# Shift and scale of the adaptive norm as dot products on VectorE over turned weights, in a four-layer fp32 kernel

## The chip, the cores and the metric

One core of one Trainium2 chip. The metric is the device time of one execution in microseconds (us), as the median of several runs.

## The reference, cut to what matters

Four layers follow one another on x of 256 x 1024 in fp32: layer 0 (stick-breaking attention and an S5 mixer), layer 1 (gated linear attention, GLA), and two hybrid layers (dilated attention and retention), called layers 2 and 3 here. Only the hybrid layers are modulated by a vector c of 1024 elements:

```python
c_act = jax.nn.silu(c)
for l in range(DEPTH):            # DEPTH = 2: layers 2 and 3
    mod = c_act @ w_ada[l] + b_ada[l]          # w_ada[l]: 1024 x 3072
    shift, scale, gate = jnp.split(mod, 3, axis=-1)
    h = rmsnorm(x, norm_w[l]) * (1.0 + scale[:, None, :]) + shift[:, None, :]
    proj = h @ w_in[l]
    ...
    x = x + gate[:, None, :] * (merged @ w_out[l])
```

Neither c_act nor w_ada depends on x, so the three parts of mod can be computed at any time before their use: shift and scale before the layer's first projection, the gate before its residual.

## The kernel before, in words

All large products use a split of fp32 in two: a matrix W is WH + WL, with WH = W rounded to the matmul's fp32r form and WL = W - WH, and likewise the activations (HTh, HTl or YTh, YTl). A product is three matmuls: high by high, low by high, high by low. The weights come in 306 **pieces** of 256 rows by 512 columns (512 KB; some of layer 1 have 336 or 352 columns). SP loads a piece into one of five RAW buffers; ScalarE copies it to WH (`hi`, line 1046), VectorE subtracts to WL (`lo`, line 1523), TensorE multiplies (`half`, lines 593 to 605; `split_half`, lines 631 to 633, where a layer opens or closes). WH and WL have three buffers each: `hi(n)` waits until TensorE has read piece n-3, and runs two pieces ahead.

The clock of the whole program is the half piece, here a **step**: piece n is steps 2n and 2n+1. Each engine is written as one loop over the steps, and tables (`AT_...`) say at which step an engine does a side job. All engines thus keep one order, and an engine waits where another is late. SP's loop is set against the same steps. Steps up to 107 are layer 0, from 108 layer 1; layers 2 and 3 each have 216 steps, counted from 0 again within the layer. A side job on VectorE at a step stands ahead of that step's `lo`.

The modulation is such a side job. Its weights are read as they lie, 128 rows (of the 1024) by 512 columns at a time, 256 KB:

- A **step of the modulation** multiplies a 128x512 block of w_ada by a column of c_act (one number per partition) and adds it to an accumulator of 128x512. Eight steps make a column group (cg). Groups 0 and 1 are shift, 2 and 3 scale, 4 and 5 gate.
- In layers 0 and 1, VectorE does groups 0 and 2 for layer 2 (`ada0`, lines 1915 and 1918, 16 steps at `AT_ADA0`), and GpSimd does groups 1 and 3 (`ada`, lines 2372 to 2376, a multiply and an add as two instructions, 16 steps at the same places). SP loads VectorE's blocks (line 2484, three buffers), GpSimd its own (line 2360, two buffers).
- In layers 2 and 3, GpSimd does the rest (`LATER`: both gate groups for layer 2, then all six groups for layer 3), 64 steps at `AT_ADA1`: 48 in layer 2, at steps 8 to 194, and 16 in layer 3, at steps 16 to 66.
- The accumulator's 128 partitions must then be summed. TensorE does it (`ada_sum`). For shift and scale it needs the result as a column: four matmuls with the accumulator as weights and one column of ones (line 814). For the gate it needs the result in all partitions: one matmul with the 128x128 ones as weights (line 817).
- VectorE takes the sums from PSUM and adds b_ada (`ada_out`, lines 1926 to 1936). ScalarE applies shift and scale as it copies the turned norm (`Bcols`, `Acols`).

The rest that the text below names: line 1696/1698, the product behind the GLU; line 1962, the logarithm's part of GLA's decay; line 2001, GLA's gating, whose result TensorE turns (line 556); lines 2068 and 2098/2102, the gating of the attention and of the retention; L1853 is the scan of S5.

```python
AT_ADA0 = (82, 86, 90, 94, 98, 112, 116, 120) + tuple(130 + 4 * i for i in range(8))
AT_ADA0_SUM = {126: (0, 1), 164: (2, 3)}
```

Of the kernel before, what the change touches and what calls it, by code (L numbers as in the profile page):

```python
# [11 lines left out]
ALU = mybir.AluOpType  # L12
# [3 lines left out]
P = 128  # L16
# [93 lines left out]
AT_ADA0_SUM = {126: (0, 1), 164: (2, 3)}  # L110
# [12 lines left out]
LATER = [(0, 4), (0, 5)] + [(1, cg) for cg in range(6)]  # L123
AT_ADA1 = tuple(8 + 29 * g + 3 * k + (0, 20, 50)[g // 2 - 1 if g > 3 else 0] for g in range(8) for k in range(8))
AT_ADA1_SUM = tuple(35 + 29 * g + (0, 20, 50)[g // 2 - 1 if g > 3 else 0] for g in range(8))


def program(nc, t, out):
    ctx = ExitStack()
    with ctx:  # L130
# [21 lines left out]
        CS = sb("CS", [P, 2, 256])  # L152
        SM = sb("SM", [P, 952])
# [97 lines left out]
        ADA = [AH.take(3, 512), AH.take(2, 512)]  # L251
        ADACC = AH.take(2, 512)
# [23 lines left out]
        HN32 = flat(OR).rearrange("p (a b) -> p a b", a=8)  # L276
        SC, PT, ATD = A2.take(1152), A2.take(1152), A2.take(384)
# [126 lines left out]
        def raw_landed(n):  # L404
# [6 lines left out]
         l_fw) = (sem(n) for n in ("l_cols l_ci l_cr l_pos l_br l_tri l_sbm l_gm l_res l_wg l_atm l_dec "  # L411
                                   "l_g0 l_g1 l_fw").split())
        s_ada = [sem(f"ada{i}") for i in range(5)]
# [71 lines left out]
        CACT, CACT_V = events("cact", ["th"]), events("cact_v", ["c"])  # L485

        ADA_V = events("ada_v", range(16))
        ADA_P = events("ada_p", [(l, i) for l in range(2) for i in range(16 + 48 * l)])
        MOD = events("mod", [(0, cg) for cg in range(6)] + [(1, cg) for cg in range(6)])
# [36 lines left out]
        def tensor_program():  # L526
# [277 lines left out]
            def ada_sum(l, cg):  # L804
                late = (l, cg) in LATER
                acc = ADACC2 if late else ADACC[:, cg % 2, :]
                ps = take(("ada", l, cg), MOD.of(l, cg))
                if late:
                    pe.wait_ge(*ADA_P.of(1, 8 * LATER.index((l, cg)) + 7))
                else:  # L810
                    pe.wait_ge(*(ADA_P.of(0, 4 * cg + 3) if cg % 2 else ADA_V.of(4 * cg + 7)))
                if cg < 4:
                    for c in range(4):
                        ins = nc.tensor.matmul(ps[:, c:c + 1], acc[:, 128 * c:128 * c + 128], ONES[:, 0:1], start=True,
                                               stop=True)
# [179 lines left out]
            for time in range(2 * groups["zr"]["at"] + 6, 2 * H0[0]):  # L995
# [5 lines left out]
                if time in AT_ADA0_SUM:  # L1001
                    for cg in AT_ADA0_SUM[time]:
                        ada_sum(0, cg)
# [10 lines left out]
            for l in range(2):  # L1014
                open_layer(2 + l, 2 * H0[l])
                for time in range(6, 216):
                    half(2 * H0[l] + time)
                    if 216 * l + time in AT_ADA1_SUM:
                        ada_sum(*LATER[AT_ADA1_SUM.index(216 * l + time)])
# [24 lines left out]
        def scalar_program():  # L1044
# [22 lines left out]
            def turned(l, ti, r):  # L1067
# [4 lines left out]
                for k in (2 * r, 2 * r + 1):  # L1072
# [4 lines left out]
                    else:  # L1077
                        act.wait_ge(*MOD.of(l - 2, 3))
# [303 lines left out]
            for time in range(2 * groups["zr"]["at"] - 6):  # L1382
# [75 lines left out]
            act.wait_ge(*side("ada", 0, 3))  # L1458
# [58 lines left out]
        def vector_program():  # L1517
# [389 lines left out]
            def ada0(i):  # L1907
                cg, k = 2 * (i // 8), i % 8
                dve.wait_ge(s_ada[i % 3], 16 * (i // 3 + 1))
                w, acc = ADA[0][:, i % 3, :], ADACC[:, 0, :]  # L1910
                if k == 0:
                    dve.wait_ge(*CACT_V.of("c"))
                    if i:
                        dve.wait_ge(*side("ada", 0, cg - 2))
                    ts(acc, w, cact[:, 0:1], None, ALU.mult).then_inc(*dve.mark(ADA_V, i))
                else:
                    dve.wait_ge(*ADA_V.of(i - 1))
                    stt(acc, w, cact[:, k:k + 1], acc, ALU.mult, ALU.add).then_inc(*dve.mark(ADA_V, i))
# [222 lines left out]
            for time in range(2 * groups["zr"]["at"] - 6):  # L2141
# [42 lines left out]
                for b, c in AT_SB_TURN.get(time, ()):  # L2184
                    yt_lo(4 * b + c, "sb", b, c)
# [428 lines left out]
```

## Time and profile before

| what | value |
|---|---|
| median of 3 runs | 1083.46 us (1083.02 to 1085.13) |
| the profiled execution: span from first to last instruction | 1080.6 us; no separate own time is listed for it |
| granted TensorE clock, mean | 0.985 |
| busy: TensorE, VectorE, ScalarE, GpSimd | 1023.9, 703.8, 565.1, 339.1 us |
| read from HBM | 189.07 MB, 176 GB/s over the span |
| loads of w_ada | 80 by GpSimd, 16 by SP, 256 KB each |

The busy time of TensorE is that of pipelined matmuls whose ends overlap: a 128x512 matmul shows as 0.39 us while the next starts after 0.23. Start-to-start distances are the ones to add up. For VectorE, too, an instruction's end overlaps the next one's start by up to 0.1 us. Layer 0 runs to about 227 us, layer 1 to 355, layer 2 to 720.

### The profile page before, as it was taken

To read this page: it belongs to the slowest core of one execution; us is meant where nothing else is said; L and a number is where in the kernel's file an instruction comes from. 1 tells how busy PE (TensorE), PEld (TensorE's weight loads), DVE (VectorE), ACT (ScalarE), POOL (GpSimd) and SP (SyncE) were. 2 spreads that over 40 slices of the span, in tenths; PEclk is the share of its full clock that TensorE was granted. 3 is DMA by queue.
4 is the path that set the end of the run, shared out by engine and by line. 5 is a ranking of instruction groups with operands and counts; after the bars stand their busy time and mean duration, and the time that the engine had idled before them with its cause. 6 is when DMAs were issued, how large, how long until landed. Compare 5 with 4: busy or idle time off the path is not lost.

```text
span 1080.6 us, 15495 instructions
## 1 busy us (share of the span) xinstructions
PE 1023.9 (95%) x6084; PEld 899.1 (83%) x6084; DVE 703.8 (65%) x1072; ACT 565.1 (52%) x872; POOL 339.1 (31%) x349
## 2 busy tenths in 40 slices
PE   5899999989999799999999989989999999999994
PEld 5688889768978589998899878867999889988883
DVE  7884946878767664456476686674545555758665
ACT  6978577547444654455443334555444554334452
POOL 4700060423520164653363555321744000420001
PEclk9899999999999999999999999999999999999997
DMA  7543434757735487765576556646876446644541
GB/s 239 168 123 98 138 96 137 246 181 230 244 127 169 147 265 224 238 197 154 172 217 187 182 157 223 223 123 192 251 215 205 117 120 188 180 150 145 188 161 58
DMA packets 94440, 191.12 MB, mean 177 GB/s; under 512 B 6768, under 2 KB 10096, under 8 KB 94368
## 3 DMA queue, kind: packets, MB, share of 16 engines
q1 hardware_dynamic: 86256, 164.71, 49.7%
q0 software_dynamic: 6960, 22.71, 6.6%
q10 hardware_dynamic: 1152, 2.72, 0.7%
q8 instruction: 48, 0.79, 0.3%
q14 instruction: 24, 0.20, 0.1%
HBM read 189.07 MB, written 1.05 MB: 176 GB/s over the span
## 4 chain that ended last, share of the span: by engine, by line
PE 86%; DVE 7%; ACT 4%; DMA 1%; issue 1%; DVEq 0%; SPq 0%; ACTq 0%
PE G L593 15%; PE G L595 14%; PE G L594 14%; PE G L602 8%; PE G L604 8%; PE G L605 8%; DVE WL L1523 2%; PE B L556 2%; ACT AR L1046 1%; ACT WH L1046 1%; DMA RAW<-in_even_w_in 1%; PE G L631 1%; PE G L633 1%; PE G L632 1%; PE B L905 1%
## 5 line engine op out<-in xcount | busy, mean ns | idle before, releaser
L1523 DVE TENSOR_TENSOR WL<-RAW,WH 128x1024 fp32r<-128x1024 f32 (+2 forms) x306 | 396.4, 1298 | 266.8 <-ACT WH L1046 265.9
L1046 ACT ACTIVATE WH<-RAW 128x1024 fp32r<-128x1024 f32 (+2 forms) x306 | 320.3, 1050 | 289.0 <-PE G L595 148.0
L593 PE MATMUL G<-WH,HTh 128*128 128x512 f32 (+1 forms) x564 | 228.9, 406 | 6.6 <-DVE WL L1523 6.4
L602 PE MATMUL G<-HTh,WH 128*128 128x256 f32 x768 | 219.9, 286 | 0.5 <-DVE HTl L1599 0.5
L595 PE MATMUL G<-WL,HTh 128*128 128x512 f32 (+1 forms) x564 | 219.2, 389 | 0.0
L594 PE MATMUL G<-WH,HTl 128*128 128x512 f32 (+1 forms) x564 | 218.4, 387 | 0.0
L604 PE MATMUL G<-HTl,WH 128*128 128x256 f32 x768 | 217.6, 283 | 0.0
L605 PE MATMUL G<-HTh,WL 128*128 128x256 f32 x768 | 217.5, 283 | 0.0
L602 PEld LDWEIGHTS G<-HTh,WH 128*128 128x128 f32 x768 | 146.8, 191 | 2.4 <-issue 2.2
L604 PEld LDWEIGHTS G<-HTl,WH 128*128 128x128 f32 x768 | 146.9, 191 | 0.9 <-issue 0.7
L605 PEld LDWEIGHTS G<-HTh,WL 128*128 128x128 f32 x768 | 146.8, 191 | 0.0
L2360 POOL DMA_DIRECT2D AR<-in_w_ada x80 | 47.5, 594 | 273.4 <-PE G L595 160.3
L593 PEld LDWEIGHTS G<-WH,HTh 128*128 128x128 f32 x564 | 106.8, 189 | 29.9 <-DVE WL L1523 9.2
L595 PEld LDWEIGHTS G<-WL,HTh 128*128 128x128 f32 x564 | 106.4, 189 | 22.0
L594 PEld LDWEIGHTS G<-WH,HTl 128*128 128x128 f32 x564 | 106.9, 190 | 18.3 <-issue 0.2
L2376 POOL TENSOR_TENSOR AR<-AR 128x512 f32<-128x512 f32 x70 | 118.5, 1693 | 5.8
L593 PE MATMUL G<-WH,YTh 128*128 128x512 f32 x184 | 73.8, 401 | 4.5 <-DVE WL L1523 4.5
L595 PE MATMUL G<-WL,YTh 128*128 128x512 f32 x184 | 72.5, 394 | 0.0
L594 PE MATMUL G<-WH,YTl 128*128 128x512 f32 x184 | 72.3, 393 | 0.0
L2374 POOL TENSOR_SCALAR AR<-AR,SM 128x512 f32<-128x512 f32 x70 | 62.0, 886 | 19.5 <-DMA AR<-in_w_ada 13.9
L1046 ACT ACTIVATE AR<-B 128x512 f32<-128x512 f32 (+5 forms) x83 | 43.0, 546 | 44.9 <-PE B L950 22.4
L2394 POOL TENSOR_TENSOR AR<-AR 128x256 f32<-128x256 f32 x16 | 18.2, 1139 | 139.5 <-DVE AR L2022 138.4
(344 smaller groups left out, 1342.2 us busy)
## 6 DMA issues: line engine op xcount, KB each, us to landing
RAW<-in_w_in SPq DMA_DIRECT2D x176, 512.0 KB, 3.8
RAW<-in_even_w_in SPq DMA_DIRECT2D x40, 512.0 KB, 3.6
AR<-in_w_ada POOLq DMA_DIRECT2D x80, 256.0 KB, 4.1
RAW<-in_odd_w_in SPq DMA_DIRECT2D x16, 512.0 KB, 4.0
RAW<-in_w_proj_ret SPq DMA_DIRECT2D x16, 512.0 KB, 3.6
RAW<-in_w_out SPq DMA_DIRECT2D x16, 512.0 KB, 4.2
RAW<-in_even_w_out SPq DMA_DIRECT2D x12, 512.0 KB, 3.9
AR<-in_w_ada SPq DMA_DIRECT2D x16, 256.0 KB, 5.0
```

The costliest lines, as they stand in the source:

```text
L556: ins = nc.tensor.transpose(ps[:, 128 * k:128 * k + 128], src(ti, j), IDENT)
L593: nc.tensor.matmul(o, xh, wh, start=begins, stop=False)
L594: nc.tensor.matmul(o, xl, wh, start=False, stop=False)
L595: ins = nc.tensor.matmul(o, xh, wl, start=False, stop=ends)
L602: nc.tensor.matmul(o, fh, h_[:, kx, :], start=begins and f % 2 == 0, stop=False, skip_group_check=True)
L604: nc.tensor.matmul(o, fh, l_[:, kx, :], start=False, stop=False, skip_group_check=True)
L605: ins = nc.tensor.matmul(o, fl, h_[:, kx, :], start=False, stop=ends and f % 2 == 1, skip_group_check=True)
L1046: return nc.scalar.activation(out_, ps, ACT.Copy, **kw)
L1523: vt(wl, raw, wh.bitcast(F32), ALU.subtract).then_inc(*dve.mark(LO, n))
L2360: nc.gpsimd.dma_start(dst, wv[:, k, 512 * cg:512 * cg + 512]).then_inc(s_ada[3 + i % 2], 16)
L2374: gts(w, w, cact[:, k:k + 1], 0.0, ALU.mult, ALU.add).then_inc(*pool.tick())
L2376: gtt(acc, acc, w, ALU.add).then_inc(*pool.mark(ADA_P, l, i))
```

## The change

Shift and scale are computed the other way round. The host turns their 2048 columns of w_ada, so that 128 output columns lie on the 128 partitions and the 1024 inputs along the row (`w_ada_t`; one contiguous block of 128x1024, 512 KB). The row of c_act is put in all partitions once (`CB`: a load by GpSimd at step 60, Tanh on ScalarE and one product on VectorE at step 78). Then one instruction on VectorE, a multiply with a sum along the row (`tensor_tensor_reduce`, with b_ada as the start), gives 128 of the outputs as a column, where they are wanted. There are 16 such **dots** for layer 2, at the 16 steps where `ada0` stood, and 16 for layer 3, in layer 2 at steps 27 to 72, every third. GpSimd does the gates alone: 16 steps in layers 0 and 1 (the same places), 16 in layer 3 (steps 26 to 71). TensorE's sums of shift and scale go; those of the gate of layer 2 move to steps 126 and 164. SP loads for all dots, into two buffers; DOT1 uses the place of OR, which is free then. Two waits for the old sum (0, 3), on ScalarE and on GpSimd ahead of layer 2, become waits for the last turn of GLA. The scratch for GpSimd's DMA descriptors is set to 8192 bytes.

```diff
-AT_ADA0_SUM = {126: (0, 1), 164: (2, 3)}
+AT_ADA0_SUM = {126: 4, 164: 5}
...
-LATER = [(0, 4), (0, 5)] + [(1, cg) for cg in range(6)]
-AT_ADA1 = tuple(8 + 29 * g + 3 * k + (0, 20, 50)[g // 2 - 1 if g > 3 else 0] for g in range(8) for k in range(8))
-AT_ADA1_SUM = tuple(35 + 29 * g + (0, 20, 50)[g // 2 - 1 if g > 3 else 0] for g in range(8))
+AT_DOT1 = tuple(27 + 3 * i for i in range(16))
+AT_ADA1 = tuple(216 + 26 + 3 * i for i in range(16))
+AT_ADA1_SUM = {216 + 50: 4, 216 + 74: 5}
+AT_CB = 78
...
-                if cg < 4:
-                    for c in range(4):
-                        ins = nc.tensor.matmul(ps[:, c:c + 1], acc[:, 128 * c:128 * c + 128], ONES[:, 0:1], start=True,
-                                               stop=True)
-                else:
-                    ins = nc.tensor.matmul(ps[:, :], ONES, acc, start=True, stop=True)
-                ins.then_inc(*told("ada", l, cg))
+                pe.wait_ge(*ADA_P.of(l, 8 * cg - 25))
+                nc.tensor.matmul(ps[:, :], ONES, ADACC2 if l else ADACC, start=True, stop=True).then_inc(
+                    *told("ada", l, cg))
...
+                if time == AT_CB:
+                    act.wait_ge(*side("sbo", 1, 1))
+                    act.wait_ge(l_cb, 16)
+                    nc.scalar.activation(DOT0[:, 1, :], CB[:, :], ACT.Tanh, scale=0.5).then_inc(*act.mark(CACT, "row"))
...
-            act.wait_ge(*side("ada", 0, 3))
+            act.wait_ge(*side("yt", "gla", 2))
...
-            def ada0(i):
...
-                    stt(acc, w, cact[:, k:k + 1], acc, ALU.mult, ALU.add).then_inc(*dve.mark(ADA_V, i))
+            def dot(l, i):
+
+                w = (DOT1 if l else DOT0)[:, i % 2, :]
+                dst = (Bcols if i < 8 else Acols)[l][:, i % 8:i % 8 + 1]
+                dve.wait_ge(s_dot[i % 2], 16 * (8 * l + i // 2 + 1))
+                dve.wait_ge(*CACT_V.of("row"))
+                nc.vector.tensor_tensor_reduce(w, w, CB[:, :], 0.5, co[f"b_ada{l}"][:, i:i + 1], ALU.mult, ALU.add,
+                                               dst).then_inc(*dve.mark(DOT, l, i))
+                if i == 15:
+                    dve.wait_ge(*DOT.of(l, 15))
+                    stt(Acols[l], Acols[l], 1.0, co[f"norm_w{l}"], ALU.add, ALU.mult).then_inc(*dve.mark(MOD, l, "c"))
...
+                if time == AT_CB:
+                    dve.wait_ge(*CACT.of("row"))
+                    stt(CB[:, :], DOT0[:, 1, :], 1.0, CB[:, :], ALU.add, ALU.mult).then_inc(*dve.mark(CACT_V, "row"))
...
+                    if l == 0 and step in AT_DOT1:
+                        dot(1, AT_DOT1.index(step))
...
+                if time == 60:
+                    nc.gpsimd.dma_start(CB[:, :], t["c_2"].partition_broadcast(P)).then_inc(l_cb, 16)
...
+            def dot_load(l, i):
+                if i >= 2:
+                    sp.wait_ge(*DOT.of(l, i - 2))
+                elif l:
+                    sp.wait_ge(*HT_LO.of(2, 1, 3))
+                    sp.wait_ge(*ROT_A.of("sin"))
+                    sp.wait_ge(*ROT_V.of("cos"))
+                elif i:
+                    sp.wait_ge(*CACT_V.of("row"))
+                nc.sync.dma_start((DOT1 if l else DOT0)[:, i % 2, :], t["w_ada_t"][l, 128 * i:128 * i + 128, :]).then_inc(
+                    s_dot[i % 2], 16)
...
+                    if at_ in AT_ADA0 and AT_ADA0.index(at_) < 14:
+                        dot_load(0, AT_ADA0.index(at_) + 2)
+                    step = at_ - 2 * H0[0]
+                    if step == AT_DOT1[0] - 3:
+                        dot_load(1, 0)
+                        dot_load(1, 1)
+                    if step in AT_DOT1 and AT_DOT1.index(step) < 14:
+                        dot_load(1, AT_DOT1.index(step) + 2)
...
+    a["w_ada_t"] = a["w_ada_2"][:, :, 0:2048].transpose(0, 2, 1)
+    a["w_ada_g"] = a["w_ada_2"][:, :, 2048:3072]
...
-    nc = _bacc.Bacc("TRN2", target_bir_lowering=False, num_devices=1)
+    nc = _bacc.Bacc("TRN2", target_bir_lowering=False, num_devices=1, dynamic_dma_scratch_size=8192)
```

How the instructions stand then, at two places on VectorE. Names: RAW, WH, WL as above; AR is the large buffer in which the blocks and accumulators lie; SM holds columns. A dot shows as two rows named ISA, the multiply with its sum and the instruction that writes the sum. First the end of layer 0, steps 86 to 98, before:

```order
L1523 TENSOR_TENSOR WL<-RAW,WH 128x1024 x2
L1918 SCALAR_TENSOR_TENSOR AR<-AR,SM 128x512
L1696 SCALAR_TENSOR_TENSOR AR<-AR 128x512
L1698 SCALAR_TENSOR_TENSOR AR<-AR 128x512
L1696 SCALAR_TENSOR_TENSOR AR<-AR 128x512
L1698 SCALAR_TENSOR_TENSOR AR<-AR 128x512
L1523 TENSOR_TENSOR WL<-RAW,WH 128x1024
L2190 TENSOR_TENSOR YTl<-AR,YTh 128x512
```

and with the change (its own line numbers):

```order
L1521 TENSOR_TENSOR WL<-RAW,WH 128x1024 x2
L1911 ISA AR,SM<-AR,CB,SM 128x1024
L1911 ISA SM 128x1
L1694 SCALAR_TENSOR_TENSOR AR<-AR 128x512
L1696 SCALAR_TENSOR_TENSOR AR<-AR 128x512
L1694 SCALAR_TENSOR_TENSOR AR<-AR 128x512
L1696 SCALAR_TENSOR_TENSOR AR<-AR 128x512
L1521 TENSOR_TENSOR WL<-RAW,WH 128x1024
L2178 TENSOR_TENSOR YTl<-AR,YTh 128x512
```

The dot stands where the half-width step stood, ahead of the GLU's product and of the next low half. Second, layer 2 from step 17 on, before:

```order
L1523 TENSOR_TENSOR WL<-RAW,WH 128x1024 x3
L1669 TENSOR_TENSOR CS<-AR 128x256
L1671 TENSOR_SCALAR CS<-CS 128x256
L1523 TENSOR_TENSOR WL<-RAW,WH 128x1024 x6
L1936 TENSOR_TENSOR AR<-B,AR 128x512
L1523 TENSOR_TENSOR WL<-RAW,WH 128x1024 x15
```

and with the change, up to the third dot:

```order
L1521 TENSOR_TENSOR WL<-RAW,WH 128x1024 x3
L1667 TENSOR_TENSOR CS<-AR 128x256
L1669 TENSOR_SCALAR CS<-CS 128x256
L1521 TENSOR_TENSOR WL<-RAW,WH 128x1024 x2
L1911 ISA AR,SM<-AR,CB,SM 128x1024
L1911 ISA SM 128x1
L1521 TENSOR_TENSOR WL<-RAW,WH 128x1024 x2
L1911 ISA AR,SM<-AR,CB,SM 128x1024
L1911 ISA SM 128x1
L1521 TENSOR_TENSOR WL<-RAW,WH 128x1024
L1911 ISA AR,SM<-AR,CB,SM 128x1024
L1911 ISA SM 128x1
```

Here VectorE had only low halves and two sums to fetch; now a dot follows each one or two low halves.

## Rows read from the trace of the kernel before

A row of the timeline has the start and the duration in us, the engine, the line, the operation, out<-in, the sizes and how many it merges; in brackets the idle time before it and what ended it. A row of waits has the total in us, the times and the longest. A row of groups has the count, the busy us and mean ns of one, and the idle us before it. A row of windows has the stretch, its length, then the busy us of TensorE, its weight loads, VectorE, ScalarE and GpSimd, the granted clock, the DMA share and GB/s.

**Rows 1.** Page, busy times by engine, and the chain by engine.

```profile
PE 1023.9 (95%) x6084; PEld 899.1 (83%) x6084; DVE 703.8 (65%) x1072; ACT 565.1 (52%) x872; POOL 339.1 (31%) x349
...
PE 86%; DVE 7%; ACT 4%; DMA 1%; issue 1%; DVEq 0%; SPq 0%; ACTq 0%
```

**Rows 2.** Waits, TensorE, whole span; total us, times, longest.

```profile
PE B L556 <- DVE AR L2068: 0.8, 1, 0.8
```

**Rows 3.** Timeline, TensorE: the sums of shift and scale.

```profile
334.57 1.84 PE L814 MATMUL B<-CI,AR 128*128 128x1 f32 x16
...
336.59 0.39 PE L594 MATMUL G<-WH,YTl 128*128 128x512 f32 x1
```

**Rows 4.** Timeline, TensorE: one sum of a gate, layer 3.

```profile
831.76 1.02 PE L817 MATMUL B<-AR,CI 128*128 128x512 f32 x2
...
832.85 0.40 PE L594 MATMUL G<-WH,HTl 128*128 128x512 f32 x1
```

**Rows 5.** Timeline, GpSimd, VectorE, TensorE: steps 90 to 98.

```profile
205.01 2.15 POOL L2376 TENSOR_TENSOR AR<-AR 128x512 f32<-128x512 f32 x1
...
205.93 1.78 DVE L1918 SCALAR_TENSOR_TENSOR AR<-AR,SM 128x512 f32<-128x512 f32 x1
...
213.38 0.50 PE L593 MATMUL G<-WH,YTh 128*128 128x512 f32 x1 [1.75 <-DVE WL L1523]
...
215.59 0.74 DVE L1918 SCALAR_TENSOR_TENSOR AR<-AR,SM 128x512 f32<-128x512 f32 x1
216.25 2.87 DVE L1523 TENSOR_TENSOR WL<-RAW,WH 128x1024 fp32r<-128x1024 f32 x2
```

**Rows 6.** Groups by form, VectorE: prices of near instructions.

```profile
L1853 DVE TENSOR_TENSOR_SCAN YF<-AR,YF 128x1024 f32<-128x1024 f32 x2 | 4.6, 2284 | 0.0
...
L1890 DVE SCALAR_TENSOR_TENSOR AR<-AR 128x768 f32<-128x768 f32 x4 | 3.7, 950 | 2.3 <-ACT AR L1188 2.3
...
L1574 DVE TENSOR_SCALAR SM<-SM 128x1 f32<-128x1 f32 x10 | 1.4, 144 | 0.0
```

**Rows 7.** Timeline, VectorE and TensorE: steps 112 to 126.

```profile
248.49 1.21 DVE L1523 TENSOR_TENSOR WL<-RAW,WH 128x1024 fp32r<-128x1024 f32 x1
...
250.00 0.48 PE L593 MATMUL G<-WH,HTh 128*128 128x512 f32 x1
...
260.13 1.23 DVE L1962 SCALAR_TENSOR_TENSOR AR<-AR 128x1024 f32<-128x1024 f32 x1 [0.23 <-ACT AR L1286]
...
265.87 2.35 DVE L1523 TENSOR_TENSOR WL<-RAW,WH 128x1024 fp32r<-128x1024 f32 x2
...
267.67 0.40 PE L593 MATMUL G<-WH,HTh 128*128 128x512 f32 x1
```

**Rows 8.** Timeline, VectorE and TensorE: steps 154 to 158.

```profile
320.59 1.78 DVE L1918 SCALAR_TENSOR_TENSOR AR<-AR,SM 128x512 f32<-128x512 f32 x1
...
327.16 0.63 PE L556 MATMUL B<-CI,AR 128*128 128x128 f32 x4 [1.66 <-DVE AR L2001]
...
331.64 1.21 DVE L1523 TENSOR_TENSOR WL<-RAW,WH 128x1024 fp32r<-128x1024 f32 x1
...
333.12 0.47 PE L593 MATMUL G<-WH,YTh 128*128 128x512 f32 x1
```

**Rows 9.** Timeline, layer 2; window of the same place in layer 3.

```profile
639.32 3.92 DVE L1523 TENSOR_TENSOR WL<-RAW,WH 128x1024 fp32r<-128x1024 f32 x2
...
641.07 0.50 PE L593 MATMUL G<-WH,YTh 128*128 128x512 f32 x1 [2.74 <-DVE WL L1523]
...
996.00:1060.00 64.00, 63.88 (x297) 52.61 (x296) 40.88 (x50) 31.54 (x42) 0.00 (x0) 1.00 0.48 156
```

**Rows 10.** Window of part of layer 2; timeline, VectorE, in it.

```profile
400.00:480.00 80.00, 80.00 (x631) 77.76 (x630) 39.54 (x35) 37.33 (x42) 42.65 (x44) 1.00 0.74 228
...
447.42 1.23 DVE L1523 TENSOR_TENSOR WL<-RAW,WH 128x1024 fp32r<-128x1024 f32 x1 [1.35 <-ACT WH L1046]
```

**Rows 11.** Loads of w_ada, issue to landing.

```profile
DMA to landing us min/median/max: 2.9/4.2/7.3
```

More of the change, by code:

```diff
@@ L250, in program @@
         AH = Arena(2048)
-        ADA = [AH.take(3, 512), AH.take(2, 512)]
-        ADACC = AH.take(2, 512)
+        DOT0 = AH.take(2, 1024)
+        ADA = AH.take(2, 512)
+        ADACC = AH.take(512)
         A1 = Arena(1024)
@@ L410, in program @@
         (l_cols, l_ci, l_cr, l_pos, l_br, l_tri, l_sbm, l_gm, l_res, l_wg, l_atm, l_dec, l_g0, l_g1,
-         l_fw) = (sem(n) for n in ("l_cols l_ci l_cr l_pos l_br l_tri l_sbm l_gm l_res l_wg l_atm l_dec "
-                                   "l_g0 l_g1 l_fw").split())
-        s_ada = [sem(f"ada{i}") for i in range(5)]
+         l_fw, l_cb) = (sem(n) for n in ("l_cols l_ci l_cr l_pos l_br l_tri l_sbm l_gm l_res l_wg l_atm l_dec "
+                                   "l_g0 l_g1 l_fw l_cb").split())
+        s_ada, s_dot = ([sem(f"{n}{i}") for i in range(2)] for n in ("ada", "dot"))
         s_out = [sem(f"out{i}") for i in range(4)]
@@ L484, in program @@
         GLU_V = events("glu_v", L2)
[L485 to L489, printed above, removed]
+        CACT, CACT_V = events("cact", ["th", "row"]), events("cact_v", ["c", "row"])
+        DOT = events("dot", [(l, i) for l in L2 for i in range(16)])
+        ADA_P = events("ada_p", [(l, i) for l in L2 for i in range(16)])
+        MOD = events("mod", [(0, 4), (0, "c"), (0, 5), (1, "c"), (1, 4), (1, 5)])
         GLA_R = events("gla_r", L2)
@@ L1001, in tensor_program @@
                 if time in AT_ADA0_SUM:
-                    for cg in AT_ADA0_SUM[time]:
-                        ada_sum(0, cg)
+                    ada_sum(0, AT_ADA0_SUM[time])
                 if time in AT_GLA["keys"]:
@@ L1018, in tensor_program @@
                     if 216 * l + time in AT_ADA1_SUM:
-                        ada_sum(*LATER[AT_ADA1_SUM.index(216 * l + time)])
+                        ada_sum(1, AT_ADA1_SUM[216 * l + time])
                     if time in AT_ATT["scores"]:
@@ L2192, in vector_program @@
                 if time in AT_ADA0:
-                    ada0(AT_ADA0.index(time))
+                    dot(0, AT_ADA0.index(time))
                 if time % 2:
@@ L2204, in vector_program @@
                 if time in AT_ADA0_SUM:
-                    for cg in AT_ADA0_SUM[time]:
-                        ada_out(0, cg)
+                    ada_out(0, AT_ADA0_SUM[time])
                 if time == AT_GLA["scan"]:
@@ L2209, in vector_program @@
                 if time in AT_ADA0:
-                    ada0(AT_ADA0.index(time))
+                    dot(0, AT_ADA0.index(time))
                 if time in AT_GLA["scores"]:
@@ L2237, in vector_program @@
                     if 216 * l + step in AT_ADA1_SUM:
-                        ada_out(*LATER[AT_ADA1_SUM.index(216 * l + step)])
+                        ada_out(1, AT_ADA1_SUM[216 * l + step])
+                    if l == 0 and step in AT_DOT1:
+                        dot(1, AT_DOT1.index(step))
                     if step in AT_ATT["scores"]:
```

71 lines of the change are left out of this document (18 added, 53 removed).

## The prediction

> **What bounds the kernel now.** I read the page's busy shares and its chain first, then TensorE's waits, then the timelines of TensorE, VectorE and GpSimd wherever the change adds or removes work. TensorE is busy 1023.9 of 1080.6 us and carries 86% of the chain, VectorE 7% [rows 1]. So an instruction taken from TensorE is worth its full length wherever TensorE finds its next piece of weights ready, and nothing where it would then wait for it. Work added to VectorE costs only where the low half (WL) of a piece arrives late: look at how long before the first matmul of a piece its L1523 ends. "Slack" below is that distance.
>
> All stretches come from one execution with a span of 1080.6 us. The page gives no separate time of its own for it. The median of three runs is 1083.46 us, 2.9 us above the span; I take those 2.9 us as unchanged and apply the difference to the median.
>
> **1. Column sums removed from TensorE.** The shift and scale sums are 8 groups of 4 matmuls; a group of 4 shows as 8 records, since two groups show as 16 [rows 3]: 64 records in all. These 16 stand from 334.57, and the second matmul behind them starts at 336.59, against 0.23 us per matmul elsewhere: 2.02 - 0.23 = 1.79 us, or 0.112 per record. Times 64: **7.1 us**. The four gate sums stay. Two of them move from layer 2 to steps 126 and 164; each costs 832.85 - 831.76 - 0.23 = 0.86 us [rows 4], the same in both places. So step 126 gives 1.79 - 0.86 = 0.93, step 164 the same, layer 2 the other 5.3 us.
>
> At step 126 almost nothing of it arrives. The next piece starts at 267.67, and its WL comes out of a pair of L1523 that begins at 265.87; the first ends near 267.04 [rows 7]: slack 0.63. VectorE is the hurried engine there (logarithm, scan, product), and the dot of step 120 makes it later by 0.65 less the 0.23 us that it idles ahead of L1962 at 260.13 [rows 7]: 0.42. Left over is 0.63 - 0.42 = 0.2 of the 0.93. **Loss 0.8 us.** At step 164 VectorE itself waits for TensorE's turns of GLA, and in layer 2 for the high halves (part 4); there the gain stays.
>
> **2. What a dot costs on VectorE.** No two-source multiply with a sum along the row is in the trace. Below: as a plain two-source instruction, L1523 of 128x1024 in 1.23 us [rows 10], with a free read of the sum. Above: the scan L1853 of 128x1024, 2.28 us [rows 6], plus 0.14 for the second instruction that writes the sum (nearest row L1574, 144 ns). I take 1.23 + 0.14, since L1890, also two inputs from SBUF but with two operations, runs at the plain rate (768 elements in 950 ns) [rows 6]; the scan feeds each result back before the next element, which a plain sum may or may not do. An old step of half the width holds VectorE for 216.25 - 215.59 = 0.66 us. Next starts overlap ends by about 0.1, so a dot holds it for some 1.3: **+0.65 to 0.7 us** per dot in layers 0 and 1; the upper bound would be +1.7.
>
> The Trainium skill, page "Vector Engine (DVE) Microarchitecture Reference", section "7. Points that are easy to get wrong", says that this family of instruction runs at half throughput with two SBUF sources that are not bf16, because no read port is left for the accumulator. For the form without a sum L1890 contradicts it; for the form with a sum no row here decides. By that rule the sum below would end near no change; this is a rival below.
>
> Beside a GpSimd step VectorE waits: the old step took 1.78 us from 205.93, with GpSimd's L2376 running from 205.01, and 0.74 alone at 215.59 [rows 5]. GpSimd keeps its steps at the same places in layers 0 and 1, so this wait is in both kernels, and only the longer body counts.
>
> **3. Where that shows.** Step 90: GELU's gate and the next WL stand behind the dot, and TensorE already waits 1.75 us at 213.38 [rows 5]: +0.7. Steps 94 and 98: the pair of L1523 from 216.25 [rows 5] is ahead of its two pieces by over 1 us, as the pieces take 2.7 us each and the first of them began at 213.38 + 2 x 2.8 = 219: nothing. Step 112: the L1523 at 248.49 ends at 249.70, TensorE takes it at 250.00 [rows 7]: 0.7 - 0.3 = +0.4. Steps 130 to 150: the dots follow at 5.8 us, two pieces of weights (2.5 us) and one dot beside GpSimd (2.4 us) fill 4.9 of it: nothing. Step 154: the dot stands ahead of the rstd and the gating that TensorE waits for at 327.16 [rows 8]: +0.7. Step 158: WL from 331.64 ends at 332.77 and is used at 333.12 [rows 8]: 0.65 - 0.35 = +0.3. **Together +2.1 us.** The c row at step 78 (one Tanh on ScalarE, one 1.2 us product on VectorE) comes ahead of the first dot; before it VectorE has neither a GpSimd step nor a wait of TensorE beside it, so I give it 0, and 1.2 us as its other end.
>
> **4. Dots of layer 2, steps 27 to 72.** From 400 to 480 us VectorE is busy 39.5 of 80 us; ahead of the L1523 at 447.42 it idles 1.35 us [rows 10]. ScalarE's high half starts when the piece three back has been read; two pieces of 2.88 us follow it, less 1.06 for the high half, 1.23 for the low one and 0.1 of handing over: a low half is some 3.3 us early. Sixteen dots of 1.3, one in one and a half pieces (4.3 us), go into that: **0**. If the cover is gone, the excess over 3.3 us shows. The queue: SP issues each load behind the dot two before it, 6 steps or 8.6 us ahead of use; loads of w_ada land in 2.9 to 7.3 us, median 4.2 [rows 11]. DMA works at 0.74 of its time with 228 GB/s there [rows 10]. 512 KB per 4.3 us in place of 256 KB brings about 290 to 305 GB/s, near the 308 that 228/0.74 gives. I take no wait, with this as a rival. The five pieces of RAW in flight cover a few us of lateness.
>
> **5. GpSimd leaves layer 2.** Its 48 steps there go. Behind one of them VectorE's pair of L1523 took 3.92 us at 639.32, and TensorE waited 2.74 us at 641.07 [rows 9]. The wait of 0.8 for L2068 [rows 2] has the same neighbour. In layer 3, same code and no GpSimd steps at those places, L2068 is waited for not once (the count in rows 2 is 1 for both layers), and TensorE is busy 63.88 of 64 us where the other stood [rows 9]. So **-3.5 us**; bounds 0 and -3.5. ScalarE and GpSimd now wait for the last turn of GLA rather than for a sum 5 steps earlier; ScalarE has passed that turn anyway and nothing behind it is due before layer 2.
>
> Sum: -7.1 + 0.8 + 2.1 - 3.5 = -7.7, so **1075.8 us**. With dots at their upper end it loses some 8 us more (rival A); with no loss at all it is -10.6 (1072.9).
>
> **Rivals.**
> A, half-rate dots: each +1.7 instead of +0.7. Step 90 1.7; 94 and 98 1.0; 112 1.4; 120 0.85 beyond losing the 0.93; 134 to 150 about 2.0, since the slack of 1.4 and the idle time are overrun; 154 1.7; 158 1.35: 10.0. Gains 6.2 + 3.5. Result +0.3: **1083.8**. For it the scan's 2.28 us, against it L1890. Layer 2 stays covered (2.4 is under 3.3).
>
> B, the loads become the wait: place steps 27 to 72. Two buffers, so two dots take one landing L plus 1.3; seven such rounds against 8.6 us each. If contention makes L 10 us, 7 x 2.7 = 19, less 3.3 slack, 15.7 lost: 1083.5 - 7.7 + 15.7 = **1091.5**, slower than before. It turns the sign from L = 8.9 us. For it: 305 GB/s near what the DMA share allows. Against: the longest landing is 7.3 us.
>
> C, VectorE already rules layers 0 and 1 and layer 2 gives less: both sums' 1.9 lost there instead of 0.8, the losses 4.1 instead of 2.1 (two more places like those named), and 0.8 of the 3.5 us coming back as another wait: -7.1 + 1.9 + 4.1 - 2.7 = -3.8, **1079.7**. For it: the three slacks under 0.7 us [rows 7, 8]. Against it: TensorE shows no wait between 240 and 327 us but for those named, so most places have some slack left.
>
> **How the numbers follow.** Chances: forecast 0.65, A 0.13, B 0.07, C 0.15. The measurement tells 0.2%, 2.2 us, from no change. Forecast and most of C are faster, with a bit of A: 0.77. A and the weak end of C: same 0.12. B and the bad half of A: slower 0.11. The range takes the forecast's best end with 1 us beyond it, C, and A: 1071.5 to 1085.0; B's bulk is left out.
>
> **What would show it.** No L814; TensorE about 7 us less busy with an equal number of weights; dots of 1.2 to 1.3 us alone and 2.3 beside GpSimd; the wait at step 90 near 2.4 us; none near 641 and 555; in layer 2 VectorE still idle before L1523; ada_t loads landing under 7 us. It is wrong if a dot alone takes over 2 us, if TensorE waits for WL between steps 27 and 75, or if the wait behind GLA grows by more than 1.5 us.

## The result, and the profile after

| | before | after |
|---|---|---|
| median of the runs, us | 1083.24 (1081.86 to 1085.13, 4 runs) | 1071.50 (1070.94 to 1072.12, 4 runs) |
| ratio to before, 95% interval | | 0.989 (0.9869 to 0.9911) |
| profiled execution: span, us | 1080.6 | 1069.3 (own time 1071.09) |
| mean granted clock of TensorE | 0.985 | 0.986 |

The change is faster by 11.7 us, where 7.7 were predicted; the time lies at the lower edge of the range. A later group of four runs of the same kernel, on the chip of the last experiments, gave 1069.00 (ratio 0.9874, 0.9857 to 0.9890). Below, "the changed kernel" with a time is the first of these groups, and "as run again" the second.

The page of the changed kernel: busy time by engine, the chain by engine, then the groups of the new instructions and the landing time of their loads.

```profile
PE 1019.7 (95%) x6020; PEld 894.4 (84%) x6020; DVE 709.5 (66%) x1111; ACT 566.0 (53%) x873; POOL 201.0 (19%) x212
...
PE 86%; DVE 8%; ACT 4%; issue 1%; DMA 1%; DVEq 0%; ACTq 0%
...
L1911 DVE CUSTOM_DVE_ANT_0 AR<-AR,CB,SM 128x1024 f32<-128x1024 f32 x32 | 48.4, 1514 | 2.9 <-DMA AR<-in_w_ada_t 2.9
...
AR<-in_w_ada_t SPq DMA_DIRECT2D x32, 512.0 KB, 4.8
```

Against [rows 1], TensorE issues 64 matmuls fewer, GpSimd is busy 138 us less, and VectorE only 5.7 us more, though its 32 dots take 48.4 us where its 14 multiply-and-add steps of layers 0 and 1 took 19.7: the same 306 subtractions for WL take 383.3 us in place of 396.4, with fewer GpSimd instructions beside them. The loads of the dots land in 4.8 us (3.7 to 7.9), a little above the 4.2 of [rows 11]; VectorE waited for one of them once, 2.9 us, with nothing of TensorE's behind it.

What a dot costs, by its line (columns: durations min/median/max in ns, first and last start):

```profile
L1911 DVE CUSTOM_DVE_ANT_0 AR<-AR,CB,SM x32: 1271/1280/2319, 196.7 to 475.0; 128x1024 f32<-128x1024 f32 x32
L1911 DVE DVE_READ_ACCUMULATOR2_ANT SM<- x32: 74/80/86, 197.9 to 476.2; 128x1 f32 x32
```

Alone it takes 1.28 us, next to the 1.23 that was taken, and 0.08 for reading the sum out. So two fp32 sources from SBUF with a sum ran at the rate of the plain two-source instruction here.

TensorE's waits over the whole span, the five largest (us in total, times, longest):

```profile
PE B L699 <- DVE TK L1586: 17.1, 8, 10.8
PE G L598 <- DVE WL L1521: 8.8, 6, 3.7
PE G L636 <- DVE HTl L1601: 5.6, 4, 1.7
PE G L636 <- DVE HTl L1597: 2.7, 2, 2.0
PE B L561 <- DVE AR L1986: 2.0, 1, 2.0
```

The wait for the gating of the attention [rows 2] is gone, and so is the one of 2.74 us at 641 [rows 9]. The wait behind GLA's gating was 1.66 [rows 8] and is 2.0 here (L1986 is what was L2001). Timeline of the place of step 90, GpSimd, VectorE, TensorE:

```profile
205.84 2.15 POOL L2363 TENSOR_TENSOR AR<-AR 128x512 f32<-128x512 f32 x1
...
206.76 2.32 DVE L1911 CUSTOM_DVE_ANT_0 AR<-AR,CB,SM 128x1024 f32<-128x1024 f32 x1
...
211.68 1.59 POOL L2363 TENSOR_TENSOR AR<-AR 128x512 f32<-128x512 f32 x1
...
212.05 2.29 DVE L1521 TENSOR_TENSOR WL<-RAW,WH 128x1024 fp32r<-128x1024 f32 x1
...
214.40 0.50 PE L598 MATMUL G<-WH,YTh 128*128 128x512 f32 x1 [1.94 <-DVE WL L1521]
```

The dot from 206.76 ends 1.09 us after GpSimd's product ends (207.99), the L1521 from 212.05 ends 1.07 after GpSimd's (213.27). Each looks as if it had begun its own 1.2 us only when GpSimd's two-source instruction was done. In [rows 5] the half-width step ends 0.55 us after GpSimd's. Both traces show it each time: the seven dots that start while an L2363 runs all end 1.08 to 1.09 us after it, and the nine half-width steps of before 0.55 to 0.56 after L2376. The other way round, a GpSimd instruction that starts while VectorE runs an L1521 ends 1.13 to 1.17 us after that, and takes 1.3 us where nothing is beside it. So at this place a dot holds VectorE 0.5 us longer than the half-width step, as its width says; the wait at step 90 still went only from 1.75 to 1.94, since the low half behind the dot again stands behind an instruction of GpSimd in both kernels.

Where the two executions drift apart, by the start of TensorE's 306 pieces (after minus before, us, at the time of the piece in the kernel before):

```
208.8 (ahead of step 90)               +0.84
331.1 (behind steps 90 to 158)         +3.33
337.7 (step 164)                       +2.32
385.7 (layer 2 under way)              +0.97
529.6 (three sums gone)                -1.42
568.7 (a fourth, the waits for L2068, L2102)   -3.34
635.4                                  -3.34
641.1 (the wait of 2.74 gone)          -6.25
654.0 (the clock behind it, a fifth)    -8.96
696.8 (the sixth sum)                  -10.02
731.6 (layer 3 begins)                 -8.43
1060.8 (last pieces)                   -8.40
```

The stream of pieces gained 8.4 us; the spans differ by 11.3. The other 2.9 us lie behind the last piece, in the end of the program. Last issue of an output, on ScalarE's queue, of before and then of after; the spans end at 1080.6 and 1069.3:

```profile
1075.00 0.35 ACTq L1513 DMA_DIRECT2D out<-X  x1
```

```profile
1066.56 0.35 ACTq L1511 DMA_DIRECT2D out<-X  x1
```

5.6 us before, 2.7 after. The theory to test: the sums gave what they were priced at, GpSimd's leaving layer 2 gave the waits and a stretch at half clock behind them, and the rest is the end of the program, by the smaller descriptor scratch.

### The profile page after: what moved, and what is told of

It reads as the page before. It is cut to its first block, busy times and chain, and to the rows that moved or that the text cites. A ratio compares the mean times of both kernels' runs of the same rounds, so it can differ in the third digit from the quotient of the medians.

```text
span 1069.3 us, 15213 instructions
## 1 busy us (share of the span) xinstructions
PE 1019.7 (95%) x6020; PEld 894.4 (84%) x6020; DVE 709.5 (66%) x1111; ACT 566.0 (53%) x873; POOL 201.0 (19%) x212
## 4 chain that ended last, share of the span: by engine, by line
PE 86%; DVE 8%; ACT 4%; issue 1%; DMA 1%; DVEq 0%; ACTq 0%
PE G L598 15%; PE G L600 14%; PE G L599 14%; PE G L607 8%; PE G L610 8%; PE G L609 8%; DVE WL L1521 2%; PE B L561 2%; ACT AR L1040 1%; ACT WH L1040 1%; DVE AR L1911 1%; PE G L636 1%; PE G L638 1%; PE G L637 1%; PE B L900 1%
## 5 line engine op out<-in xcount | busy, mean ns | idle before, releaser
L1521 DVE TENSOR_TENSOR WL<-RAW,WH 128x1024 fp32r<-128x1024 f32 (+2 forms) x306 | 383.3, 1255 | 251.7 <-ACT WH L1040 250.6
L2347 POOL DMA_DIRECT2D AR<-in_w_ada_g x32 | 19.0, 593 | 171.5 <-PE G L610 63.4
L1911 DVE CUSTOM_DVE_ANT_0 AR<-AR,CB,SM 128x1024 f32<-128x1024 f32 x32 | 48.4, 1514 | 2.9 <-DMA AR<-in_w_ada_t 2.9
L2363 POOL TENSOR_TENSOR AR<-AR 128x512 f32<-128x512 f32 x28 | 49.8, 1779 | 2.3
```

What stands on the lines that cost most here:

```text
L1521: vt(wl, raw, wh.bitcast(F32), ALU.subtract).then_inc(*dve.mark(LO, n))
L1911: nc.vector.tensor_tensor_reduce(w, w, CB[:, :], 0.5, co[f"b_ada{l}"][:, i:i + 1], ALU.mult, ALU.add, dst).then_inc(*dve.mark(DOT, l, i))
L2347: nc.gpsimd.dma_start((ADA2 if l else ADA)[:, i % 2, :], wv[:, i % 8, 512 * (i // 8):512 * (i // 8) + 512]).then_inc(s_ada[i % 2], 16)
L2363: gtt(acc, acc, w, ALU.add).then_inc(*pool.mark(ADA_P, l, i))
```

## The experiments

Twelve kernels ran, in three groups of four, each group on one chip with the kernel before beside it (medians 1082.86, 1082.81 and 1083.41).

### 1. The kernel before once more

No edit. 

> The kernel before, unchanged, once more with a profile. Between the two traces the stretch from ScalarE's last output DMA (1075.00 before, 1066.56 after) to the end of the span shrank from 5.6 to 2.7 us: 2.9 of the 11.3 us by which the spans differ, with no work of the change near it. If that end belongs to the program before, it is 5.6 us here again. If it was a chance of one execution, it is 2.7 here and the span is about 1077.7.

Measured: 1085.13 in its one run, span 1083.3, and the end of the program again 1083.3 - 1077.74 = 5.6 us. Against the first profile of the same kernel its pieces run 1.45 us late from 79 us on and 2.4 us late from 641 on, where TensorE waited 3.40 us instead of 2.74. So places of the waits and of the half-clock stretches differ by 1 to 2.5 us between executions of one kernel; the 5.6 us at the end don't.

### 2. The smaller scratch alone

```diff
-    nc = _bacc.Bacc("TRN2", target_bir_lowering=False, num_devices=1)
+    nc = _bacc.Bacc("TRN2", target_bir_lowering=False, num_devices=1, dynamic_dma_scratch_size=8192)
```

on the kernel before. 

> The kernel before with the scratch for GpSimd's DMA descriptors at 8192 bytes as in the change, nothing else. Theory S (the end of the program depends on the scratch): the stretch behind the last output DMA is 2.7 us and the time 1080.5. Rival N (it goes with the number of GpSimd's instructions or DMAs, or is chance): no change, 1083.3, and an end of 5.6 us as in the profile before, or one that varies from run to run.

Measured: 1081.41 (1078.33 to 1083.27, 10 runs), ratio 0.9982 (0.9971 to 0.9993). Span and last output:

```profile
core 0: 1079.8 us, clock 0.981
```

```profile
1077.09 0.35 ACTq L1513 DMA_DIRECT2D out<-X  x1
```

2.71 us behind the last issue instead of 5.6. This is the line of the diff that the prediction gave no term. The four profiles with the default scratch all show 5.6, the ten with a smaller one 2.7. The runs give 1.5 us of medians and an interval of 0.8 to 3.1; the profile gives 2.9 at the place.

The traces also show what stands there. When GpSimd's last instruction is issued, its queue goes into a DRAIN, and the program closes only when that one and SP's are both done (SP's follows the landing of the last output). First the kernel before, then this one (columns: durations min/median/max in ns, first and last start):

```profile
L130 POOLq DRAIN  x1: 8562/8562/8562, 1071.8 to 1071.8; - x1
L130 SPq DRAIN  x1: 7/7/7, 1077.5 to 1077.5; - x1
```

```profile
L130 POOLq DRAIN  x1: 2927/2927/2927, 1073.9 to 1073.9; - x1
L130 SPq DRAIN  x1: 7/7/7, 1079.6 to 1079.6; - x1
```

Before, GpSimd's DRAIN takes 8.56 us and ends 2.9 us after SP's; with the smaller scratch it takes 2.93 us here and 4.72 in the changed kernel, ends first, and SP's is the last.

### 3. GpSimd made small in layer 2, nothing else

```diff
+                if l and i < 48 and k:
+                    gts(acc[:, 0:8], w[:, 0:8], cact[:, k:k + 1], 0.0, ALU.mult, ALU.add).then_inc(
+                        *pool.mark(ADA_P, l, i))
+                    return
```

on the kernel before. 

> The kernel before, in which 42 of GpSimd's 48 steps in layer 2 are one instruction of 8 columns in place of a multiply and an add of 512 (their loads, waits and signals stay; gates of layer 2 and shift and scale of layer 3 are therefore not computed). Theory W (GpSimd's wide steps hold up VectorE, TensorE then waits at L2068 and at the low half behind the retention, and its clock falls to half for 3.4 us after the long wait): the waits of 0.8 and 2.7 us go, and about 1.9 us more from the clock: 1083.3 - 5.4 = 1077.9. Rival (only the waits count, as I forecast): 1079.8. Rival (those waits come from elsewhere): 1083.

Measured: 1076.86 (1075.18 to 1077.39, 4 runs), ratio 0.9943 (0.9928 to 0.9958). TensorE waits nowhere between 380 and 710 us. Windows of before and then of this kernel behind the place of the wait (columns: us; busy us and count of PE, PEld, DVE, ACT, POOL; granted clock; DMA share; GB/s):

```profile
640.00:644.00 4.00, 2.93 (x9) 2.34 (x10) 4.00 (x5) 0.00 (x0) 2.14 (x1) 0.78 0.37 131
644.00:648.00 4.00, 3.78 (x18) 2.66 (x18) 3.97 (x6) 1.46 (x5) 0.00 (x0) 0.79 0.39 133
```

```profile
640.00:644.00 4.00, 4.00 (x23) 3.39 (x22) 4.00 (x9) 3.85 (x9) 0.00 (x0) 1.00 0.38 132
644.00:648.00 4.00, 4.00 (x23) 3.44 (x22) 3.35 (x7) 1.48 (x2) 1.30 (x2) 1.00 0.55 152
```

Before, the clock fell from 2.4 to 1.2 GHz for part of these 8 us, after TensorE had stood for 2.74; without the wait it stays at 2.4. The pieces gain 1.0 us at L2068 (waits of 0.8 and 0.2) and 4.8 across this place, 2.1 more than the wait itself. This is the second thing that the sum lacked.

### 4. One column in each sum instead of four

```diff
-                    for c in range(4):
-                        ins = nc.tensor.matmul(ps[:, c:c + 1], acc[:, 128 * c:128 * c + 128], ONES[:, 0:1], start=True,
-                                               stop=True)
+                    ins = nc.tensor.matmul(ps[:, 0:1], acc[:, 0:128], ONES[:, 0:1], start=True, stop=True)
```

on the kernel before. 

> The kernel before, in which each column sum of shift and scale is one matmul in place of four (the other three columns repeat the first, so shift and scale are not the reference's). It takes 48 of the 64 records away, 0.112 us each, 5.4 us. Of 12 of these at step 126 (1.35 us) only 0.63 can arrive, as the low half is late there: -4.6, so 1078.7. Rival (column sums run in gaps of TensorE's stream and cost less than their distance): 1081 to 1083.

Measured: 1079.73 (1078.22 to 1086.8, 10 runs), ratio 0.9981 (0.9966 to 0.9996). In layer 2 the pieces step back by 0.64 to 0.69 us at each sum. A sum with 6 of its 8 records gone should give 6 x 0.112 = 0.67. So a record's 0.112 holds, and arrives in full at the four column sums of layer 2, where TensorE isn't waiting.

### 5. Layer 2's gate taken out of layers 0 and 1

```diff
-AT_ADA0_SUM = {126: 4, 164: 5}
+AT_ADA0_SUM = {}
+LATER = [(0, 4), (0, 5), (1, 4), (1, 5)]
+AT_ADA1 = (tuple(7 + 3 * i for i in range(8)) + (98, 101, 104, 107, 118, 121, 124, 127)
+           + tuple(216 + 26 + 3 * i for i in range(16)))
-AT_ADA1_SUM = {216 + 50: 4, 216 + 74: 5}
+AT_ADA1_SUM = {31: (0, 4), 130: (0, 5), 216 + 50: (1, 4), 216 + 74: (1, 5)}
```

on the changed kernel, with the indices that follow from it. 

> The changed kernel with the 16 GpSimd steps of layer 2's gate taken out of layers 0 and 1 and put into layer 2 (steps 7 to 28 and 98 to 127 of it), their sums at steps 31 and 130 of layer 2. Theory: beside a GpSimd step a dot takes 2.3 us in place of 1.28, and the waits of TensorE at step 90 (2.0 us) and at step 154 (the longest, 1.9 us) stand behind such steps; both shrink to near 0, and some of the half-clock stretch after step 154 goes with them. 1071.5 - 2.0 - 1.9 = 1067.6, down to 1066 with the clock. Rival 1: VectorE's own work sets those waits, and without GpSimd it only shifts; 1071. Rival 2: the steps cost in layer 2 what they gave up before; 1070 to 1072, with a wait of TensorE on VectorE between 390 and 560 us.

Measured: 1072.10 (1069.35 to 1072.69, 5 runs), ratio 0.9892 (0.9873 to 0.9910): no gain in sum. By pieces, against the changed kernel, it gained 7.6 us from step 90 to the end of layer 1 (1.7 of it the two sums, which only moved), lost 1.4 at the sum of step 31, and then 7.7 at one place. TensorE there, and two windows around it:

```profile
570.32 0.28 PE L612 MATMUL G<-HTh,WL 128*128 128x256 f32 x1
575.63 2.08 PE L814 MATMUL B<-AR,CI 128*128 128x512 f32 x2 [5.04 <-POOL AR L2366]
```

```profile
570.00:575.00 5.00, 0.59 (x5) 0.39 (x4) 1.23 (x1) 0.32 (x1) 4.65 (x6) 1.00 0.72 214
575.00:580.00 5.00, 4.37 (x18) 3.33 (x19) 0.69 (x1) 0.20 (x1) 0.58 (x1) 0.66 0.16 59
```

The sum of step 130 waits for GpSimd, whose steps stand in line with its rotations of the retention (8 instructions between 555.9 and 573.0). This is neither rival: it is a wait for my new order. 5.04 us of waiting cost 7.7, since the clock fell behind it.

### 6. GpSimd made small in layers 0 and 1

```diff
+                elif l == 0:
+                    gts(acc[:, 0:8], w[:, 0:8], cact[:, k:k + 1], 0.0, ALU.mult, ALU.add).then_inc(
+                        *pool.mark(ADA_P, l, i))
```

on the changed kernel, in place of the product and the sum. 

> The changed kernel with 14 of the 16 GpSimd steps of layers 0 and 1 reduced to 8 of 512 columns and to one instruction (the gate of layer 2 is not computed), DMAs and semaphores kept. Theory: the contention of GpSimd with VectorE in layers 0 and 1 costs the waits at steps 90 and 154, 3.9 us together: 1067.6. Rival: the longer dots alone cost them; then 1071, and the waits stand where they stood.

Measured: 1062.76 (1061.97 to 1063.40, 4 runs), ratio 0.9811 (0.9792 to 0.9829), 8.7 below the changed kernel, and 6.2 below it as run again, where 3.9 were expected. Between 190 and 345 us TensorE's waits on WL fall from 2.4 to 1.0 us, and the one behind GLA's gating (2.0) is gone. The pieces show 2.1 us at step 90, 0.4 to 0.5 at each of three places between 244 and 293 where no wait of 0.2 us or more is listed, and 3.3 around step 154, where the clock had fallen too, 0.8 of it given back behind: 5.7 us in layers 0 and 1. The rest is half-clock stretches placed otherwise, 0.6 at the start and 1.6 between layers 2 and 3. The theory was right on the cause; it counted only the waits that the table lists, and left the small ones and the clock out.

### 7. Dots of layer 2 done twice

```diff
+                if l:
+                    nc.vector.tensor_tensor_reduce(w, w, CB[:, :], 0.5, co[f"b_ada{l}"][:, i:i + 1], ALU.mult,
+                                                   ALU.add, dst).then_inc(*dve.tick())
+                    dve.wait_ge(*dve.prev)
```

> The changed kernel with each of the 16 dots that run in layer 2 done twice (shift and scale of layer 3 are wrong by it). Theory: they lie in VectorE's slack of some 3.3 us per piece; 2.7 us a pair fits, so 1071.5 within 1 us. Rival: the slack is smaller than read, and the excess shows at many of 16 places; 0.5 to 1.35 us each, 1079 to 1093, with waits of TensorE on WL between 410 and 490 us.

Measured: 1069.61 (1068.83 to 1073.25, 4 runs), ratio 0.9881 (0.9858 to 0.9904), so not slower. Window of layer 2, changed kernel and this one:

```profile
377.00:550.00 173.00, 171.68 (x1129) 157.07 (x1129) 106.41 (x133) 88.38 (x120) 0.00 (x0) 1.00 0.68 216
```

```profile
377.00:550.00 173.00, 172.73 (x1136) 157.79 (x1136) 124.67 (x168) 87.33 (x119) 0.00 (x0) 1.00 0.68 216
```

VectorE is busy 18 us more and TensorE loses 0.65 us by its pieces. The 0 for the dots of layer 2 stands. That the kernel came out 1.9 us below the changed one is not the edit's: 1.2 us of it are there before any dot, and the changed kernel itself did as well when run again (number 11).

### 8. Dots of layers 0 and 1 over half their elements

```diff
-                nc.vector.tensor_tensor_reduce(w, w, CB[:, :], 0.5, ...
+                n = 1024 if l else 512
+                nc.vector.tensor_tensor_reduce(w[:, 0:n], w[:, 0:n], CB[:, 0:n], 0.5, ...
```

> The changed kernel with the 16 dots of layers 0 and 1 over 512 of their 1024 elements (shift and scale of layer 2 are incomplete), so 0.53 us less each on VectorE. Theory by the pieces' start times: the longer body costs only some 0.8 us there in all, so 1070.7. Rival, the prediction's own sum: 2.1 us by the longer body and most of the 0.8 at step 126, so 1069. Rival 2: nothing, 1071.5.

Measured: 1067.88 (1067.48 to 1068.88, 4 runs), ratio 0.9861 (0.9840 to 0.9883), 3.6 below the changed kernel of its first group and 1.1 below it as run again. At step 90 the wait of 1.94 went and one of 1.23 came a piece later. By pieces the kernel gains 2.5 us from step 90 to 164, and loses 1.3 again near 370 us, where a half-clock stretch falls on busy pieces. The reading of 0.8 was too low; the prediction's 2.1, with some of the 0.8 lost at step 126, is what the pieces show.

### 9 and 10. The gate's second sum later, and the scratch smaller still

```diff
-AT_ADA1_SUM = {31: (0, 4), 130: (0, 5), 216 + 50: (1, 4), 216 + 74: (1, 5)}
+AT_ADA1_SUM = {31: (0, 4), 150: (0, 5), 216 + 50: (1, 4), 216 + 74: (1, 5)}
```

on number 5. 

> As gates_out_of_layers_0_1, with the second gate sum of layer 2 at step 150 instead of 130. Theory: there TensorE waited 5.0 us at L814 for GpSimd (whose steps lie between its rotations) and lost another 2.7 us in the half-clock stretch behind; both go, since the last GpSimd step ends some 10 us ahead of step 150: 1072.1 - 7.7 = 1064.4, within 1.5 us. Rival: the half-clock stretch comes elsewhere and only the wait goes: 1067. Rival 2: the work of GpSimd holds VectorE up in layer 2 as it did in layers 0 and 1, 1069 or more.

Measured: 1066.03 (1064.18 to 1066.46, 4 runs), ratio 0.9839 (0.9824 to 0.9853). The same timeline of VectorE, ahead of step 90, has the dots alone:

```profile
205.53 1.28 DVE L1913 CUSTOM_DVE_ANT_0 AR<-AR,CB,SM 128x1024 f32<-128x1024 f32 x1
...
209.39 1.22 DVE L1523 TENSOR_TENSOR WL<-RAW,WH 128x1024 fp32r<-128x1024 f32 x1
```

and TensorE doesn't wait there. The 5.0 us at L814 and the fall of the clock behind them are gone too. It leaves nothing out, and beats both kernels. The time is 1.6 above the 1064.4 that was expected and 1.0 below the 1067 of the first rival; the medians don't part the two.

Number 10 is number 9 with `dynamic_dma_scratch_size=4096`. 

> As gates_moved_sum_late, with 4096 bytes of descriptor scratch instead of 8192. Theory: the end of the program after the last output took 5.6 us with the default size and 2.7 us with 8192, in every profile, since something at the end grows with that size; if in proportion, 4096 gives another 1.5 us less. Rival: 2.7 us is what the last output's DMA takes, and nothing changes.

Measured: 1064.13 (1062.63 to 1066.10, 4 runs), ratio 0.9828 (0.9810 to 0.9846). The intervals of 9 and 10 overlap. Its end of the program takes 1061.6 - 1058.86 = 2.7 us, as with 8192, though GpSimd's DRAIN is down to 1.78 us: the rival holds, the landing of the last output rules, and nothing more is to be had there. By the pieces 10 is ahead of 9 at three places by half-clock stretches alone.

### 11. The changed kernel once more

No edit. 

> The changed kernel once more, on the chip of this group. 1071.5 within 0.7 us. What it tells: how far the half-clock stretches fall elsewhere from one execution to the next, so how much of the 1.9 us that dots_twice_layer2 won with more work is chance.

Measured: 1069.00 (1068.19 to 1071.63, 4 runs), 2.5 below the first group, outside of the 0.7 expected. The pieces of the two profiles part at the first wait of the program. Window there in the first profile and in this one:

```profile
50.00:55.00 5.00, 4.79 (x11) 3.79 (x12) 4.96 (x6) 4.09 (x7) 0.00 (x0) 0.50 0.64 193
```

```profile
50.00:55.00 5.00, 5.00 (x17) 3.93 (x16) 4.96 (x5) 4.55 (x7) 0.00 (x0) 0.66 0.67 210
```

1.2 us by 68 us, nothing more up to 326, 0.5 around 330; the two profiled executions differ by 1.4. So a good part of the 2.5 us between the groups is the placing of half-clock stretches, and a term of 1 us can't be read from medians, only from pieces.

### 12. Dots of layers 0 and 1 done twice

As number 7, with `if not l`. 

> The changed kernel with each of the 16 dots of layers 0 and 1 done twice (shift and scale of layer 2 are wrong by it), 1.35 us more on VectorE each. Theory: there, unlike in layer 2, VectorE is ahead of TensorE by less than 0.7 us at steps 90, 112, 120, 154, 158 and by about 1 us at 94 and 98; the excess arrives: 1.35 x 5 + 0.4 x 2 + some 3 us over steps 130 to 150 = 10.5, so 1082. Rival: idle time of VectorE between takes most of it, under 1076.

Measured: 1088.30 (1085.50 to 1089.21, 4 runs), ratio 1.0043 (1.0026 to 1.0060), slower than before. TensorE's waits of this kernel between 190 and 345 us, then those of the changed one:

```profile
PE G L598 <- DVE WL L1521: 9.0, 5, 4.9
PE G L636 <- DVE HTl L1597: 2.2, 2, 2.0
PE B L837 <- DVE AR L1942: 2.1, 1, 2.1
```

```profile
PE G L636 <- DVE HTl L1597: 2.7, 2, 2.0
PE G L598 <- DVE WL L1521: 2.4, 2, 1.9
PE B L699 <- DVE TK L1586: 2.2, 2, 1.5
PE B L561 <- DVE AR L1986: 2.0, 1, 2.0
```

21.6 us of added work on VectorE cost the pieces 20.4 us between steps 90 and 164, nearly one for one, the granted clock over these 155 us falling from 0.98 to 0.91. The expectation of 10.5 us summed the slacks place by place. It left out the clock, and that VectorE may not catch up between one step and the next; the run doesn't part the two.

## Why the prediction was right and wrong

The forecast of -7.7 us was too small by 4.0. Each part, as predicted and as the pieces show it:

| part | predicted | measured |
|---|---|---|
| steps 90 to 158, with what is lost at 126 | +2.0 | +2.5 |
| step 164 | -0.9 | -1.0 |
| sums that leave layer 2 | -5.3 | -5.1 |
| waits at L2068 and at 641 | -3.5 | -3.7 |
| clock behind the latter | none | -2.1 |
| end of the program | none | -2.9 |
| other places of half-clock stretches | none | +0.8, -1.3, +1.6 |
| sum | -7.7 | -11.2 |

The sum is added up rightly but for two roundings: the loss at step 126 is 0.93 - 0.2 = 0.7 rather than 0.8, and the range's lower end, the best end of 1072.9 "with 1 us beyond it", would be 1071.9 rather than 1071.5.

**1, the sums.** Right: 0.112 us per record (number 4), in full in layer 2 and at step 164. At step 126, 0.2 of the 0.93 us arrives, as forecast: the changed kernel's pieces are 1.41 us late at 262 us and 1.22 at 270. The sign given for the sums did not come: TensorE's busy time fell by 4.2 us and not by 7, and there are 64 weight loads fewer too.

**2, the dot.** Right: 1.28 + 0.08 us. So rival A falls, but its price was too low as well. A adds 1.0 us to each of 16 dots and asked 10.0 - 2.1 = 7.9 us for it. Number 12 adds 1.35 and loses 20.4; an estimate in proportion is 20.4 x 1.0/1.35 = 15 us, so half-rate dots would have ended at some 1084 to 1087 (from the 1069.0 and 1071.5 of the changed kernel), no faster than before. No run tests that proportion. The Trainium skill, page "Vector Engine (DVE) Microarchitecture Reference", section "7. Points that are easy to get wrong", says that an instruction of the form S2S2D2_STT runs at half throughput with two SBUF sources that are not bf16. The trace lists the dot as CUSTOM_DVE_ANT_0 and doesn't show whether it has that form; its 1280 ns show that it doesn't run at half, as the prediction's "this family of instruction" would have had it.

**3, VectorE in layers 0 and 1.** Right within 0.5 us in sum, not in its places. Step 90 moved by 0.2 instead of 0.7, because there VectorE stood behind GpSimd in either kernel, and pieces behind step 112 lost the difference. The row of c_act at step 78 cost nothing, as forecast: the pieces move by under 0.1 us between 60 and 208 us. Rival C was half right: VectorE does rule there (number 12), but the change added little to it.

**4, dots of layer 2.** Right: 0, and still 0.65 with twice the work (number 7). Rival B falls: one wait for a load, 2.9 us, and no piece late by it, though the longest landing was 7.9 us where the sign asked for under 7.

**5, GpSimd leaves layer 2.** Right in the waits (a third, of 0.2 us for L2102, was not in the sum), and the step that failed in size: "So **-3.5 us**; bounds 0 and -3.5". The profile before had the granted clock at 0.78 and 0.79 in the 8 us behind the wait at 641. With the wait went this too, 5.8 us in all (number 3), beyond the bound of 3.5.

**What was left out.** The sum has no term for the scratch size, which is in the diff, and "I take those 2.9 us as unchanged" looked at what lies around the span and not at what lies at its end. 5.6 us behind the last output were in the trace of before. That they go with the scratch, by GpSimd's DRAIN, is shown by number 2; why that takes 8.56 us with the default is open, and 4096 bytes gain nothing over 8192 (number 10). The two missing terms are -5.0 together, more than the whole error of 4.0; half-clock stretches elsewhere gave 1.1 back in this pair of executions.

## What to carry to other kernels

Price a wait that goes with the granted clock in the stretch behind it: here 2.7 us of standing cost 4.8, and 5.0 cost 7.7. Work for VectorE is free in one stage and costs nearly one for one in another of the same kernel, so ask of each place how far ahead the engine is, and whether it catches up before the next one. Go through every line of a diff, a constructor's argument too, and read the end of the span as a stage of its own.

## What the runs showed of the hardware that was not expected

- A `tensor_tensor_reduce` of 128x1024 in fp32, both sources in SBUF, shows as two instructions on VectorE, 1280 and 80 ns.
- VectorE's instruction with two sources, begun beside GpSimd's, ends about 1.08 us after GpSimd's at full width (all seven such dots) and 0.55 at half width (all nine such steps), and GpSimd's, begun beside VectorE's, 1.13 to 1.17 us after that: the two take turns whole, rather than sharing. A dot takes 2.3 instead of 1.28 us. Making GpSimd's steps small in layers 0 and 1 gave 5.7 us there (number 6).
- The end of the program, from the last output's issue, took 5.6 us with the default descriptor scratch and 2.7 with 8192 or 4096 bytes. GpSimd's closing DRAIN took 8.56 us with the default, 2.93 to 4.73 with 8192 and 1.78 with 4096; with 8192 and 4096 it ends before SP has seen the last output land, so it costs nothing.
- Nearly all half-clock stretches begin in or just behind waits of TensorE of 0.9 us or more (near 67 us two executions have one behind a wait of 0.7 or less), and they fall in other places from one execution to the next: two groups of runs of one kernel differed by 2.5 us in their medians.
